# Sliding-window attention in a fused encoder layer: 128 key slots for every query chunk, weights divided before their transposes, values as the stationary operand with 64 columns

## The chip, the cores and the metric

One core of one Trainium2 chip. The metric is the device time of one execution in microseconds, as the median of several runs. TensorE multiplies, ScalarE and VectorE do the elementwise work, GpSimd makes constants at the start, SyncE issues the weight transfers. Everything is float32; the large products are made of rounded float32 parts (fp32r), one pass each, the small ones in plain float32, two passes each (transposes one).

## The reference, cut to what matters

One layer over 256 positions of width 2048: an input projection, a gated recurrence, the attention below, an output projection, an MLP, a gated embedding, norms. The change touches the attention alone.

```python
def swa_sink_attention(q, k, v, sinks, cos, sin):
    ...
    kb = band_blocks(k.reshape(B, N, CHUNK, ATT_KV_HEADS, ATT_HEAD_DIM), N)
    vb = band_blocks(v.reshape(B, N, CHUNK, ATT_KV_HEADS, ATT_HEAD_DIM), N)
    s = jnp.einsum('bnqhgd,bnkhd->bnhgqk', q, kb).astype(jnp.float32) * (ATT_HEAD_DIM ** -0.5)
    ...
    sink = jnp.broadcast_to(...)
    pr = jax.nn.softmax(jnp.concatenate([s, sink], axis=-1), axis=-1)[..., :-1].astype(v.dtype)
    o = jnp.einsum('bnhgqk,bnkhd->bnqhgd', pr, vb)
    return o.reshape(B, S, ATT_WIDTH)
...
merged = jnp.concatenate([jax.nn.sigmoid(gate_a) * o_a, jax.nn.sigmoid(gate_b) * o_b], axis=-1)
```

CHUNK is 64, a query sees the keys of its own chunk and of the one before (the first chunk only its own). There are 32 query heads of width 64 and 4 key and value heads, eight query heads to each.

## The kernel before, in words

**The stream.** All weights pass through TensorE in chunks of 2 x 128 rows by 512 columns. SyncE loads a chunk into one of 4 raw slots. ScalarE rounds it to `w_hi` (L893), VectorE makes the rest `w_lo` (L1220), and TensorE does 12 matmuls of 512 columns with it: four L641 and four L642 in turn (`w_hi` with the high and the low part of the activations), then four L647 (`w_lo`). There are 588 chunks; blocks of 8 or 4 chunks fill one pair of accumulators. ScalarE may split chunk n once TensorE has used chunk n-4, so each split waits for TensorE and the chunks follow each other without a gap as long as nothing is late.

**The steps.** All else is hung on that stream by a list of turns written out by hand: `steps(n)` on each engine. TensorE does the steps of turn n behind chunk n. ScalarE does them behind its split of chunk n+3 and VectorE behind its `w_lo` of chunk n+3 (`LAG` is 3). Every engine executes strictly in its written order, so a step that waits holds up all that is behind it, the splits too.

**The attention.** The 32 query heads are done in 4 groups j, each with one key head and in 8 units u: query tile t = u // 4 (128 queries, that is two chunks) and a pair of heads. Unit u of a group starts at turn `a = 4u + 4` of the group:

- a = 4u+4: TensorE, `scores` (L686). The stationary operand is `qT` of the two heads (128 columns are the 128 queries), the moving one `kTp`, in which the key head lies twice, each copy zero in the rows of the other head. Tile 0 sees keys 0 to 127 (256 moving columns), tile 1 keys 64 to 255 (384).
- a = 4u+5: VectorE, `score_max` (L1309, L1314, L1316), a reduction for each half of the rows, then the larger of it and the sink, negated. ScalarE, `exponentials` (L947), one for each half of the rows and head, four in all, into `pr0` or `pr1`.
- a = 4u+7: TensorE, `weights_turn` (L699), two transposes of 128x128 in tile 0, four in tile 1.
- a = 4u+8: VectorE copies them to `pT` (L1372).
- a = 4u+9: TensorE, `weighted_values` (L710), `pT` stationary, the values `vaug` moving with 64 columns and a 65th of ones that gives the sum of the weights.
- a = 4u+10: VectorE copies the output to `oa` (L1377).

Behind the last unit (`ATT_END`, a = 39) ScalarE makes the sinks' exponentials (L1000) and VectorE the denominators, the division and the product with the gate `sgb` (`attention_gated`, L1324 to L1330); TensorE transposes the result (`amT`), ScalarE and VectorE split it into `mT_hi` and `mT_lo` for the output projection.

The turns of TensorE share four PSUM banks; scores have bank 0, the transposed weights and the outputs of a unit bank 1. A turn waits until the one before it in its bank has been read.

**What runs beside it.** The recurrence has its steps in the same turns. Two of them matter below: its outputs (turn h = 47), where TensorE does 16 full-width matmul passes (L753), and 12 matmuls of two passes (L759) whose stationary operand has 64 columns:

```python
for h in range(HG):
    for c in (1, 2, 3):
        t, half = divmod(c, 2)
        mm = pe.matmul(bank(("o", j, t))[half * CHUNK:(half + 1) * CHUNK, h * P:(h + 1) * P],
                       qe[:, h, c * CHUNK:(c + 1) * CHUNK], Sst[:, c - 1, h, :],
```

so that c = 1 and 3 write output rows 64 to 127, c = 2 rows 0 to 63; and the split of its gated output (turn h = 62), of which VectorE's part is L1457. The latter falls among the first attention turns of the next group in group 1, in the others behind them. Turn h is counted from the block "f" of the group, a from the end of its block "gb"; both are the same chunk.

## Time and profile before

| | us |
|---|---|
| median of 3 runs | 1774.04 |
| lowest, highest | 1773.59, 1774.26 |
| span of the profiled execution | 1771.0 |
| TensorE matmuls busy | 1742.1 (98%) |
| VectorE busy | 1088.2 (61%) |
| ScalarE busy | 910.4 (51%) |

The span runs from the first to the last instruction of one profiled execution; the page gives no time of that execution besides it. The median of the runs is 3.0 us above it. Busy is the union of an engine's instructions. Matmuls overlap in the records, since each is written with its latency; the distance between the starts of two chunks, and not the mean length of a matmul, tells what one costs.

### The profile page before, as it was taken

The numbers are of one execution on the slowest core, as the hardware profiler recorded it, in microseconds if no ns is written. First come the engines' busy times: TensorE is split into PE (matmuls) and PEld (weight loads), VectorE is DVE, ScalarE is ACT, GpSimd is POOL, SyncE is SP. The second block draws the span as 40 slices with busy tenths as digits, with TensorE's granted clock in tenths as the row PEclk, the third lists the DMA queues.
The fourth block names the chain that finished last, engine by engine and source line by source line (L and its number), as shares of the span: only waits on it lengthen the run. The fifth ranks groups of instructions, "written<-read, shape, count | busy, mean of one in ns | idle before, by whom it ended". The sixth has DMA issues, their size and how long they took to land.

```text
span 1771.0 us, 22971 instructions
## 1 busy us (share of the span) xinstructions
PE 1742.1 (98%) x8357; PEld 1442.6 (81%) x8357; DVE 1088.2 (61%) x1432; ACT 910.4 (51%) x1160; POOL 21.9 (1%) x80
## 2 busy tenths in 40 slices
PE   7999999999999999999999999999999999999996
PEld 6888788888888888888888888888888888888885
DVE  6656776776657767577676455555555555555564
ACT  6556646554556545565456544444444444444453
POOL 4000000000000000000000000000000000000000
PEclk9999999999999999999999999999999999999998
DMA  6655555555655556555556666666666666666553
GB/s 217 200 171 174 155 155 177 166 160 157 188 181 163 165 155 189 180 167 160 157 184 208 188 181 192 187 192 188 189 183 194 185 191 189 191 186 184 176 185 113
DMA packets 162716, 315.33 MB, mean 178 GB/s; under 512 B 10097, under 2 KB 10418, under 8 KB 162482
## 3 DMA queue, kind: packets, MB, share of 16 engines
q1 hardware_dynamic: 161584, 312.01, 59.0%
q10 hardware_dynamic: 1026, 1.87, 0.3%
q8 instruction: 72, 1.18, 0.3%
q14 instruction: 34, 0.28, 0.1%
HBM read 311.74 MB, written 2.10 MB: 177 GB/s over the span
## 4 chain that ended last, share of the span: by engine, by line
PE 96%; DVE 1%; ACT 1%; issue 0%; DMA 0%; SPq 0%; DVEq 0%; ACTq 0%
PE acc L641 30%; PE acc L642 30%; PE acc L647 30%; PE turn L668 3%; PE turn L710 1%; PE turn L686 1%; PE turn L740 1%; PE turn L699 1%; DVE w_lo L1220 0%; ACT w_hi L893 0%; PE turn L759 0%; PE turn L753 0%; DMA w_raw<-in_w_in_dram 0%; PE turn L724 0%; DVE x_sb L1297 0%
## 5 line engine op out<-in xcount | busy, mean ns | idle before, releaser
L1220 DVE TENSOR_TENSOR w_lo<-w_raw,w_hi 128x1024 fp32r<-128x1024 f32 x588 | 719.9, 1224 | 619.3 <-ACT w_hi L893 615.5
L893 ACT ACTIVATE w_hi<-w_raw 128x1024 fp32r<-128x1024 f32 x588 | 623.1, 1060 | 699.1 <-PE acc L647 690.5
L641 PE MATMUL acc<-w_hi,hT_hi 128*128 128x512 f32 x1568 | 624.5, 398 | 6.9 <-ACT w_hi L893 3.9
L642 PE MATMUL acc<-w_hi,hT_lo 128*128 128x512 f32 x1568 | 611.9, 390 | 0.0
L647 PE MATMUL acc<-w_lo,hT_hi 128*128 128x512 f32 x1568 | 420.5, 390 | 0.0
L641 PEld LDWEIGHTS acc<-w_hi,hT_hi 128*128 128x128 f32 x1568 | 295.0, 188 | 69.5 <-ACT w_hi L893 4.3
L647 PEld LDWEIGHTS acc<-w_lo,hT_hi 128*128 128x128 f32 x1568 | 294.9, 188 | 61.8
L642 PEld LDWEIGHTS acc<-w_hi,hT_lo 128*128 128x128 f32 x1568 | 295.3, 188 | 59.1
L641 PE MATMUL acc<-w_hi,mT_hi 128*128 128x512 f32 x512 | 205.6, 401 | 0.0
L642 PE MATMUL acc<-w_hi,mT_lo 128*128 128x512 f32 x512 | 199.7, 390 | 0.0
L647 PE MATMUL acc<-w_lo,mT_hi 128*128 128x512 f32 x512 | 137.3, 390 | 0.0
L647 PEld LDWEIGHTS acc<-w_lo,mT_hi 128*128 128x128 f32 x512 | 96.1, 188 | 20.3
L641 PEld LDWEIGHTS acc<-w_hi,mT_hi 128*128 128x128 f32 x512 | 96.2, 188 | 19.7
L642 PEld LDWEIGHTS acc<-w_hi,mT_lo 128*128 128x128 f32 x512 | 96.3, 188 | 19.5
L641 PE MATMUL acc<-w_hi,aT_hi 128*128 128x512 f32 x256 | 100.7, 393 | 0.0
L642 PE MATMUL acc<-w_hi,aT_lo 128*128 128x512 f32 x256 | 100.0, 391 | 0.0
L947 ACT ACTIVATE pr<-turn,asc 64x128 f32<-64x128 f32 (+1 forms) x128 | 37.7, 343 | 96.6 <-DVE asc L1316 96.2
L647 PE MATMUL acc<-w_lo,aT_hi 128*128 128x512 f32 x256 | 69.0, 391 | 0.0
L1297 DVE TENSOR_TENSOR x_sb<-acc,x_sb 128x512 f32<-128x512 f32 x102 | 65.6, 685 | 1.8
L647 PEld LDWEIGHTS acc<-w_lo,aT_hi 128*128 128x128 f32 x256 | 48.1, 188 | 10.7
L642 PEld LDWEIGHTS acc<-w_hi,aT_lo 128*128 128x128 f32 x256 | 48.1, 188 | 10.3
L641 PEld LDWEIGHTS acc<-w_hi,aT_hi 128*128 128x128 f32 x256 | 48.1, 188 | 10.2
(210 smaller groups left out, 918.1 us busy)
## 6 DMA issues: line engine op xcount, KB each, us to landing
w_raw<-in_w_in_dram SPq DMA_DIRECT2D x232, 512.0 KB, 3.7
w_raw<-in_w_up_dram SPq DMA_DIRECT2D x128, 512.0 KB, 3.7
w_raw<-in_w_down_dram SPq DMA_DIRECT2D x128, 512.0 KB, 3.8
w_raw<-in_w_out_dram SPq DMA_DIRECT2D x64, 512.0 KB, 4.4
w_raw<-in_w_ple_gate_dram SPq DMA_DIRECT2D x32, 512.0 KB, 4.5
x_sb<-in_x_dram SPq DMA_DIRECT2D x8, 256.0 KB, 7.4
w_raw<-in_w_ple_proj_dram SPq DMA_DIRECT2D x4, 512.0 KB, 4.1
out_dram<-x_sb SPq DMA_DIRECT2D x3, 512.0 KB, 4.6
```

Source lines behind the costliest of these rows:

```text
L641: pe.matmul(a, hi[:, k, t, :], w_hi[:, s, kk, :], start=first and kk == 0, stop=False)
L642: pe.matmul(a, lo[:, k, t, :], w_hi[:, s, kk, :], start=False, stop=False)
L647: mm = pe.matmul(acc[b % 2][t][:], hi[:, k, t, :], w_lo[:, s, kk, :], start=False, stop=last and kk == 1)
L668: mm = pe.transpose(bank(name)[:, i * P:(i + 1) * P], src(i), ident[:])
L686: mm = pe.matmul(bank(name)[:, 0:2 * nk].rearrange("p (v k) -> p v k", v=2), qT[:, pair, t, :], kTp[:, j, :, k0:k0 + nk], start=True, stop ...
L699: mm = pe.transpose(bank(name)[:, i * P:(i + 1) * P], src, ident[:])
L710: mm = pe.matmul(bank(name)[:, hh * (HD + 1):(hh + 1) * (HD + 1)], pT[:, hh * (t + 1) + kt, :], vaug[:, kt, j, :], start=kt == 0, stop=kt ...
L740: mm = pe.matmul(bank(name)[:, h * P:(h + 1) * P], ke[:, h, c // 2, :], val[:, c // 2, h * P:(h + 1) * P], start=True, stop=True)
L893: act.activation(w_hi[:, n % W_SLOTS], w_raw[:, n % RAW_SLOTS], ACT.Copy)\
L947: ins = act.activation(dst, bank(name)[rows_, s0:s0 + keys], ACT.Exp, scale=HD ** -0.5, bias=asc[rows_, NM + head:NM + head + 1])
L1220: dve.tensor_tensor(w_lo[:, n % W_SLOTS], w_raw[:, n % RAW_SLOTS], w_hi[:, n % W_SLOTS].bitcast(F32), ALU.subtract).then_inc(w_lo_ready, 1)
L1297: dve.tensor_tensor(xs, acc_of(kind, j, col, t)[:], xs, ALU.add).then_inc(x_added, 1)
```

## The change

Each query chunk now has 128 key slots of its own. `kTp` has 5 pieces of 64 keys: chunks 0, 1, 2, then 1 and 3 again. For the second query chunk of tile 1 the keys are the pieces 2 and 4. The values `vv` have three tiles: the positions 0 to 127, 128 to 255, and a mixed one (the values of positions 128 to 191 in rows 0 to 63, of 64 to 127 in rows 64 to 127). `pr0` and `pr1` have 129 columns a head; the last holds the exponential of the sink. So in tile 1 every query has 128 keys: one reduction, one exponential a head over all 128 rows, two transposes.

The weights are divided before they are transposed: a new step `weights_normed` on VectorE at turn a = 4u+6 sums `pr` with the sink's column, takes the reciprocal and multiplies. TensorE's transposes wait for it (`pn_ready`) instead of for the exponentials.

The product with the values has the values stationary (64 columns) and the transposed weights moving, head 0 into rows 0 to 63 of the bank and head 1 into rows 64 to 127, so the output comes out turned (`oaT`). The gate is transposed instead of the gated output (`gbT`, turn 39 instead of 43), one product is left, and the split into `mT_hi` and `mT_lo` reads its result. The scores of tile 1 are two matmuls with 64 stationary columns.

```diff
-                k0, nk = keys_of(t)
-                mm = pe.matmul(bank(name)[:, 0:2 * nk].rearrange("p (v k) -> p v k", v=2),
-                               qT[:, pair, t, :], kTp[:, j, :, k0:k0 + nk], start=True, stop=True)
+                out_ = bank(name)[:, 0:2 * P].rearrange("p (v k) -> p v k", v=2)
+                if t == 0:
+                    mm = pe.matmul(out_, qT[:, pair, 0, :], kTp[:, j, :, 0:P], start=True, stop=True)
+                else:
+                    pe.matmul(out_[0:CHUNK], qT[:, pair, 1, 0:CHUNK], kTp[:, j, :, P:2 * P], start=True, stop=True,
+                              skip_group_check=True)
+                    late = kTp[:, j, :, P:5 * CHUNK].rearrange("p v (s c) -> p v s c", c=CHUNK)[:, :, 0:3:2, :]
+                    mm = pe.matmul(out_[CHUNK:P].rearrange("p v (s c) -> p v s c", c=CHUNK),
+                                   qT[:, pair, 1, CHUNK:P], late, start=True, stop=True, skip_group_check=True)
                 mm.then_inc(full(name), 1)
...
-                pe.wait_ge(pr_ready, 8 * j + u + 1)
+                pe.wait_ge(pn_ready, 8 * j + u + 1)
                 signal, value = bank_free(name)
                 pe.wait_ge(signal, value)
+                pr = pr0 if t == 0 else pr1
                 for hh in range(2):
-                    for kt in range(t + 1):
-                        i = hh * (t + 1) + kt
-                        src = pr0[:, hh, :] if t == 0 else pr1[:, hh, kt * P:(kt + 1) * P]
-                        mm = pe.transpose(bank(name)[:, i * P:(i + 1) * P], src, ident[:])
+                    mm = pe.transpose(bank(name)[:, hh * P:(hh + 1) * P], pr[:, hh, 0:P], ident[:])
...
-                for hh in range(2):
-                    for kt in range(t + 1):
-                        mm = pe.matmul(bank(name)[:, hh * (HD + 1):(hh + 1) * (HD + 1)],
-                                       pT[:, hh * (t + 1) + kt, :], vaug[:, kt, j, :],
-                                       start=kt == 0, stop=kt == t)
+                parts_ = ((0, slice(0, P)),) if t == 0 else ((V_MIXED, slice(0, CHUNK)), (V_LATE, slice(CHUNK, P)))
+                for v, qs in parts_:
+                    for hh in range(2):
+                        mm = pe.matmul(bank(name)[hh * HD:(hh + 1) * HD, qs], vv[:, v, j, :], pT[:, hh, qs],
+                                       start=True, stop=True, skip_group_check=True)
...
+                pr = pr0 if t == 0 else pr1
+                for hh in range(2):
+                    head = t * 8 + 2 * pair + hh
+                    act.activation(pr[:, hh, P:P + 1], sink_bc[:, 8 * j + 2 * pair + hh:8 * j + 2 * pair + hh + 1],
+                                   ACT.Exp, bias=asc[:, NM + head:NM + head + 1])
+                    for rows_, keys in parts_of(t):
+                        ins = act.activation(pr[rows_, hh, 0:keys], bank(name)[rows_, hh * P:hh * P + keys], ACT.Exp,
+                                             scale=HD ** -0.5, bias=asc[rows_, NM + head:NM + head + 1])
...
+            def weights_normed(j, u, t):
+
+                dve.wait_ge(pr_ready, 8 * j + u + 1)
+                pr, den = pr0 if t == 0 else pr1, asc[:, DEN:DEN + 2]
+                chain(dve.tensor_reduce(den, pr[:], AX_X, ALU.add))
+                chain(dve.reciprocal(den, den))
+                dve.tensor_tensor(pr[:, :, 0:P], pr[:, :, 0:P], den.unsqueeze(2).to_broadcast([P, 2, P]), ALU.mult)\
+                   .then_inc(pn_ready, 1)
...
+                        if a == UNIT * u + 6:
+                            weights_normed(j, u, t)
...
-                    if a == ATT_END + 2:
-                        dve.wait_ge(pv_out, 8 * (j + 1))
-                        dve.wait_ge(gb_sig, 2 * (j + 1))
-                        attention_gated(j)
+                    if a == ATT_END + 1:
+                        dve.wait_ge(pv_out, 8 * (j + 1))
+                        for t in range(TT):
+                            dve.wait_ge(full(("gbT", j, t)), nth(("gbT", j, t)))
+                            dve.tensor_tensor(four(sgb[:, t]), oaT[:, :, t, :], four(bank(("gbT", j, t))[:]), ALU.mult)\
+                               .then_inc(am_ready, 1)
```

Here `parts_of(t)` gives the halves of the rows with 64 and 128 keys in tile 0 and all rows with 128 keys in tile 1. Line numbers move: L1220 becomes L1226, L893 L897, L699 L703, L947 L948 with the sinks' L945, L1377 L1375; the new three are L1325 to L1327. The changes of order, as the built programs have it:

VectorE, unit 2 of group 1 (tile 0), from the bound of the scores to the recurrence's scan (`hb`); before:

```order
L1309 TENSOR_REDUCE asc<-turn 64x2 x2
L1314 SCALAR_TENSOR_TENSOR asc<-asc,sink_bc 128x2
L1316 TENSOR_SCALAR asc<-asc 128x2
L1494 TENSOR_SCALAR hk<-hf 128x512
L1220 TENSOR_TENSOR w_lo<-w_raw,w_hi 128x1024
L1377 COPY oa<-turn 128x130
L1500 SCALAR_TENSOR_TENSOR hb<-smask,hg 128x512
```

and after:

```order
L1311 TENSOR_REDUCE asc<-turn 64x2 x2
L1316 SCALAR_TENSOR_TENSOR asc<-asc,sink_bc 128x2
L1318 TENSOR_SCALAR asc<-asc 128x2
L1487 TENSOR_SCALAR hk<-hf 128x512
L1226 TENSOR_TENSOR w_lo<-w_raw,w_hi 128x1024
L1375 COPY oaT<-turn 128x128
L1325 TENSOR_REDUCE asc<-pr 128x2
L1326 RECIPROCAL asc<-asc 128x2
L1327 TENSOR_TENSOR pr<-pr,asc 128x2x128
L1493 SCALAR_TENSOR_TENSOR hb<-smask,hg 128x512
```

Three instructions have come in behind the copy of the last output, and the one that TensorE's transposes wait for is the third.

ScalarE, the exponentials of a unit of tile 0 and what stands behind them, after (before it was four of L947 in one row, in the order of the halves):

```order
L945 ACTIVATE pr<-sink_bc,asc 128x1
L948 ACTIVATE pr<-turn,asc 64x64
L948 ACTIVATE pr<-turn,asc 64x128
L945 ACTIVATE pr<-sink_bc,asc 128x1
L948 ACTIVATE pr<-turn,asc 64x64
L948 ACTIVATE pr<-turn,asc 64x128
L1060 ACTIVATE hg<-hf 128x512
```

Six instead of four, and the rows change from one to the next: all, the first 64, the last 64.

TensorE, scores of a unit of tile 1 with the recurrence's transposes behind it; before:

```order
L647 MATMUL acc<-w_lo,hT_hi 128x512 x4
L686 MATMUL turn<-kTp,qT 128x384
L668 MATMUL turn<-ident,zb 128x128 x4
L641 MATMUL acc<-w_hi,hT_hi 128x512
L642 MATMUL acc<-w_hi,hT_lo 128x512
```

and after:

```order
L647 MATMUL acc<-w_lo,hT_hi 128x512 x4
L689 MATMUL turn<-kTp,qT 64x256
L692 MATMUL turn<-kTp,qT 64x256
L668 MATMUL turn<-ident,zb 128x128 x4
L641 MATMUL acc<-w_hi,hT_hi 128x512
```

One matmul over 384 columns has become two over 256, each for half of the output rows.

## Rows read from the trace of the kernel before

**Rows 1.** The page, part 4: the chain that ended last, by engine.

```profile
PE 96%; DVE 1%; ACT 1%; issue 0%; DMA 0%; SPq 0%; DVEq 0%; ACTq 0%
```

**Rows 2.** Timeline of PE, tile 0 of group 3: start us, us, engine, line, operands.

```profile
742.37 1.07 PE L647 MATMUL acc<-w_lo,hT_hi 128*128 128x512 f32 x4
745.09 1.07 PE L647 MATMUL acc<-w_lo,hT_hi 128*128 128x512 f32 x4
...
748.07 1.09 PE L647 MATMUL acc<-w_lo,hT_hi 128*128 128x512 f32 x4
...
751.26 1.08 PE L647 MATMUL acc<-w_lo,hT_hi 128*128 128x512 f32 x4
...
754.45 1.07 PE L647 MATMUL acc<-w_lo,hT_hi 128*128 128x512 f32 x4
```

**Rows 3.** Timeline of PE, tile 1 of group 3: transposes, scores; then a values step.

```profile
809.94 1.07 PE L647 MATMUL acc<-w_lo,mT_hi 128*128 128x512 f32 x4
...
813.13 1.08 PE L647 MATMUL acc<-w_lo,hT_hi 128*128 128x512 f32 x4
...
816.52 1.07 PE L647 MATMUL acc<-w_lo,hT_hi 128*128 128x512 f32 x4
...
829.13 1.08 PE L647 MATMUL acc<-w_lo,hT_hi 128*128 128x512 f32 x4
...
832.77 1.07 PE L647 MATMUL acc<-w_lo,hT_hi 128*128 128x512 f32 x4
```

**Rows 4.** Timeline of PE, recurrence outputs of group 0; last row: the instant 240.30.

```profile
238.41 1.95 PE L753 MATMUL turn<-val,am 128*128 128x128 f32 x16
240.29 1.96 PE L759 MATMUL turn<-Sst,qe 128*64 128x128 f32 x24
...
242.52 0.39 PE L642 MATMUL acc<-w_hi,hT_lo 128*128 128x512 f32 x1
...
240.29 0.33 PE L759 MATMUL turn<-Sst,qe 128*64 128x128 f32 x2
```

**Rows 5.** Timelines of DVE, ACT and PE, unit 2 of group 3.

```profile
752.61 0.17 DVE L1316 TENSOR_SCALAR asc<-asc 128x2 f32<-128x2 f32 x1
...
752.93 1.14 ACT L947 ACTIVATE pr<-turn,asc 64x64 f32<-64x64 f32 x4 [2.60 <-DVE asc L1316]
...
757.04 0.29 DVE L1377 COPY oa<-turn 128x130 f32<-128x130 f32 x1
...
758.08 0.38 PE L699 MATMUL turn<-ident,pr 128*128 128x128 f32 x2
```

**Rows 6.** Timelines of DVE and PE: units 1, 0 and 4 of group 3, unit 0 of group 1.

```profile
743.94 0.29 DVE L1377 COPY oa<-turn 128x130 f32<-128x130 f32 x1
...
731.17 2.48 DVE L1220 TENSOR_TENSOR w_lo<-w_raw,w_hi 128x1024 fp32r<-128x1024 f32 x2 [2.43 <-ACT w_hi L893]
...
733.52 0.38 PE L699 MATMUL turn<-ident,pr 128*128 128x128 f32 x2
...
781.81 0.29 DVE L1377 COPY oa<-turn 128x130 f32<-128x130 f32 x1
...
782.85 0.60 PE L699 MATMUL turn<-ident,pr 128*128 128x128 f32 x4
...
288.06 0.69 DVE L1457 TENSOR_TENSOR mT_lo<-tmp,mT_hi 128x512 fp32r<-128x512 f32 x1 [0.48 <-ACT mT_hi L1105]
...
288.09 0.38 PE L699 MATMUL turn<-ident,pr 128*128 128x128 f32 x2
```

**Rows 7.** Groups by line and form, DVE and ACT: xcount, busy us, mean ns, idle before.

```profile
L1309 DVE TENSOR_REDUCE asc<-turn 64x2 f32<-64x256 f32 x48 | 20.4, 424 | 1.7
...
L947 ACT ACTIVATE pr<-turn,asc 64x128 f32<-64x128 f32 x96 | 29.6, 356 | 53.9 <-DVE asc L1316 53.5
...
L947 ACT ACTIVATE pr<-turn,asc 64x64 f32<-64x64 f32 x32 | 8.1, 303 | 42.7 <-DVE asc L1316 42.7
...
L1000 ACT ACTIVATE asc<-asc 128x16 f32<-128x16 f32 x4 | 0.9, 217 | 0.1
```

More of the change, by code:

```diff
@@ L974, in steps @@
                         act.wait_ge(full(("kT", i)), nth(("kT", i)))
[L975 to L977 removed]
+                        src = bank(("kT", i))[:].rearrange("p (h v c) -> p h v c", h=2, v=2)
+                        pieces = ((0, 0, 2), (1, 3, 1)) if t == 0 else ((0, 2, 1), (1, 4, 1))
+                        for c, slot_, n_ in pieces:
+                            ins = act.activation(
+                                kTp[:, 2 * half:2 * half + 2, :, slot_ * CHUNK:(slot_ + n_) * CHUNK],
+                                src[:, :, :, c * CHUNK:(c + n_) * CHUNK], ACT.Copy)
+                        ins.then_inc(kTp_out, 1)
                 for j in range(NG):
@@ L987, in steps @@
                     if a == 0:
+                        if j:
+                            act.wait_ge(moA_ready, 2 * j)
                         z_out("gb", j, sgb, gb_exp, ACT.Exp, NR)
@@ L1302, in score_max @@
                 dve.wait_ge(full(name), nth(name))
-                k0, nk = keys_of(t)
-                s = bank(name)[:, 0:2 * nk].rearrange("p (v k) -> p v k", v=2)
-                for half in range(2):
-                    rows_ = slice(half * CHUNK, (half + 1) * CHUNK)
-                    first = max(0, (2 * t + half - 1) * CHUNK) - k0
-                    end = (2 * t + half + 1) * CHUNK - k0
-                    chain(dve.tensor_reduce(asc[rows_, MX:MX + 2], s[rows_, :, first:end], AX_X, ALU.max))
+                s = bank(name)[:, 0:2 * P].rearrange("p (v k) -> p v k", v=2)
+                for rows_, keys in parts_of(t):
+                    chain(dve.tensor_reduce(asc[rows_, MX:MX + 2], s[rows_, :, 0:keys], AX_X, ALU.max))
                 head = 2 * pair
```

93 lines of the change are left out of this document (28 added, 65 removed).

## Prediction, made before the changed kernel ran

> **What bounds the kernel now.** I read the page first, then its chain of work, then the timelines of three engines in the attention turns. The chain that ended last is TensorE for 96% of the span [rows 1]. So the time is the sum of what TensorE executes plus the moments in which it waits, and every edit has one of two prices: its TensorE time, or a late operand.
>
> The price of a piece is read between chunks. A chunk ends with four L647 matmuls; from one such start to the next is 2.72 us when nothing lies between (742.37 to 745.09), and what is above 2.72 is the piece [rows 2]. In query tile 0: two transposes of weights 0.26 (2.98), scores 0.47 (3.19), values 0.47 (3.19) [rows 2]. In tile 1: four transposes 0.47 (3.19), scores over 384 columns 0.67 (3.39), values in eight passes 0.92 (829.13 to 832.77, 3.64) [rows 3].
>
> **TensorE, part by part.** There are 4 groups of 8 units, 16 units in each tile.
> The transposes of tile 1 fall from four to two: 0.47 becomes 0.26, 16 x -0.21 = -3.4 us.
> Scores of tile 0 keep their form: 0.
> Scores of tile 1 and all products with the values become 64 columns wide, in the two halves of the array. The kernel has one such step, the recurrence outputs (L759), and its price is in the trace [rows 4]. The 16 full-width L753 passes of 128 columns take 1.95 us in their row. The 24 half-width L759 passes behind them, of the same 128 columns, take 1.96; 16 of the 24 fall on the upper half and 8 on the lower. A view of the instant 240.30 has two of them from the same start, 240.29. So the halves run together, and the eight of the lower half cost nothing. A pass of 128 columns is 0.11 (two more transposes cost 0.21 [rows 2, 3]) and one of L641's 2.72/12 = 0.23. From 238.41 to the next L642 at 242.52 are 4.11; the work in it is 16 x 0.11 + 16 x 0.11 + 0.23 = 3.75. What is left, 0.35 us, is the price of a visit to the halves, going in and coming out.
> Scores of tile 1: two passes of 256 columns, 0.43, plus 0.35 = 0.78 for 0.67: 16 x 0.11 = +1.8.
> Values of tile 0: two passes of 128 columns a half, 0.22+0.35 = 0.57 for 0.47: 16 x 0.10 = +1.6.
> Values of tile 1: four passes of 64 columns a half, at 0.055 again 0.22+0.35 = 0.57 for 0.92: 16 x -0.35 = -5.6. No row has a 64-column load at this rate; at 0.11 a pass it would be 0.79. I take 0.57, since L759's loads were hidden, and keep +3.5 us for the range.
> The transposes of the gate are as many as those of the gated output that they replace: 0. The sum for TensorE is -3.4+1.8+1.6-5.6 = -5.6 us.
>
> The Trainium skill (TensorE: Matmul & The Clock Gate, "The mechanism" of Part 3) says that a load overlaps with matmuls in flight only when its row group differs. The halves here share all their rows, so by that rule they would go in turn; the trace disagrees, with the two starts at 240.29. What it would give is the third rival below.
>
> **ScalarE and VectorE, and the new wait.** The transposes of a unit (chunk 4u+7 of its group) waited for the exponentials; now they wait for VectorE's sum, reciprocal and product behind them (chunk 4u+6). All three engines are in order, so what stands before them counts: the unit's exponentials hold up the next weight split on ScalarE, that holds up VectorE's w_lo, and behind it come the copy of the last output and then the three new instructions, w_lo of the next chunks behind those.
> The new three: 0.42 (a 64x256 reduction [rows 7]; the product has 256 elements too), about 0.17 for two elements (as L1316 [rows 5]), 0.42, with 0.04 between: 1.09; to TensorE's first transpose another 0.15. ScalarE's part in tile 0: four exponentials take 1.14 [rows 5]; two sink exponentials are added (217 ns for 16 columns [rows 7]) and the order now changes the rows used at each step. A 64x128 one is 356 ns and a 64x64 one 303 [rows 7]; six one after another without overlap make 2 x (0.22+0.30+0.36) = 1.76, with some 0.01 at each joint 1.83: +0.69. If all five joints overlap by 0.1 they make 1.26: +0.12. I take +0.69: of today's four, 2 x (0.30+0.36) = 1.32 less 1.14 leaves 0.18, an overlap at two of three joints; the third is the one at which the rows change, and now every joint changes them. In tile 1 four become two of 128 columns and two sinks: shorter by about 0.3.
> Unit 0 of a group: the first w_lo ends 731.17+1.22 (half of 2.48, with its gap) = 732.40, the turn was at 733.52, 1.12 later [rows 6]. Needed are 0.69+0.03+1.09+0.15 = 1.96: TensorE waits 0.8, in three groups 2.4.
> Unit 0 of group 1: VectorE was busy with mT_lo until 288.06+0.69 = 288.75, already behind the turn at 288.09 [rows 6]; 288.75+0.69+1.09+0.15-288.09 = 2.6.
> Unit 2: last bound (L1316) 752.78, exponentials from 752.93, copy of the output done at 757.33, turn at 758.08: 0.75 left [rows 5]. Needed: 0.69+1.09-0.09+0.15 = 1.84, less 0.10 by which the longer product before it delays TensorE: 1.0, four times 4.0.
> Units 1 and 3: the copy is done at 743.94+0.29 = 744.23 and the turn follows four L647 passes of 0.23 from 745.09, at 746.0 [rows 2, 6]; 1.77 are left and 1.84 less 0.10 needed: 0.
> Unit 4: copy done 782.10, turn 782.85, 0.75 left [rows 6]; 1.15 needed and part of tile 0's lateness still there: 0.4 to 0.9, I take 0.6, four times 2.4.
> Units 5 to 7: VectorE is freed of one reduction (424 ns [rows 7]) and half a copy in each, which pays for most of the new three: 0.
> Waits: 2.4+2.6+4.0+2.4 = +11.4 us. These are what the change costs; the old tail at the end of a group (sum of denominators, 16 exponentials, four products of 512) goes, but nothing waited for it: 0. The extra pieces of kTp and values are some 0.3 us each, once, in slots where ScalarE waits for TensorE: 0. No weight transfer changes.
>
> **Sum.** 1771.0-5.6+11.4 = 1776.8 us for the span. The median of the runs (1774.04) lies 3.0 above the profiled span; the page gives no other time of that execution. So 1779.8, rounded 1780. A measurement of this kernel tells about 0.2%, 3.5 us, from no change: +6 is slower by 0.34%.
>
> **Rivals.**
> First, the new three are mostly covered: the six exponentials overlap (+0.12), so each wait of tile 0 shrinks by 0.57, 7 x 0.57 = 4.0 us, and unit 4 costs 0.4, 0.8 less. 1780-4.8 = 1775: no change that can be told. For it: two of the three joints of today's four do overlap [rows 5, 7]; against: copies then still end 0.75 before the turn.
> Second, faster: VectorE's slack holds the whole chain, TensorE never waits, and only -5.6 is left: 1768.4. It decides at 1.1 us between the copy's end and the turn; rows 5 and 6 have 0.75, which is against it. The same side is reached if visits to the halves are free: 48 x 0.35 = 16.8 us less, while 32 turns come up to 0.35 earlier and waits grow by 5 to 11: about 1770. The 0.35 around L759 is against it. The Trainium skill (TensorEngine Tiling (Array Packing), "When to Use Tiling") advises just this exchange, values stationary and two column tiles for 64 columns, for up to twice the speed; its key properties add that a change of mode drains the engine. By that gain alone the values' 0.47 and 0.92 would halve and the kernel end near 1770; the rows say that the drain eats it.
> Third, the halves go in turn: +0.43 for each scores step of tile 1, +0.22 for each product with the values, 6.9+7.0 = 13.9, less some 2 us of waits that the longer TensorE work covers: 1792. Rows 4 are against it.
> Fourth, the change could do nothing (the wait moved, all hidden, and the pieces equal): 1774. Nothing in the rows supports it.
>
> **From this the numbers.** My forecast (waits in units 0, 2 and 4) 0.62; the first rival 0.18; the second 0.10; the third 0.06; the fourth 0.04. The range reaches from the lower end of the first rival to the forecast with slow loads (+3.5) and waits larger by 0.3 in 15 places (+4.5): 1772 to 1788. Slower by over 0.2%: 0.62, the third rival and a part of the first, less the forecast's lower edge: 0.67. Within: 0.23. Faster: 0.10.
>
> **What would show it.** In the profile after: TensorE's idle time at the transposes of weights, put down to VectorE's product (L1327), about 11 us in some 13 to 16 pieces, the longest (2 to 2.6) in group 1 near 290 us; scores of tile 1 3.5 from chunk to chunk instead of 3.39, values about 3.3 in both tiles; two transposes in tile 1. The six exponentials of a tile 0 unit take 1.8. I am wrong if TensorE's waits there are under 6 us in all, or if a values step costs more than 0.7.

## The result and the profile after

The changed kernel takes 1782.65 us (median of 4 runs, 1782.08 to 1783.13) against 1773.99 us of the kernel before in the same session: the ratio is 1.005, with a 95% interval of 1.0038 to 1.0062. It is slower by half a per cent, as forecast (1780, range 1772 to 1788). The profiled execution took 1782.92 us, with a span of 1780.8, so what lies around that span is 2.1 us.

The page of the changed kernel, parts 1 and 4, which answer to [rows 1]:

```profile
PE 1741.2 (98%) x8357; PEld 1418.8 (80%) x8357; DVE 1097.0 (62%) x1492; ACT 913.7 (51%) x1194; POOL 21.8 (1%) x79
...
PE 85%; DVE 8%; ACT 4%; issue 1%; DMA 0%; ACTq 0%; SPq 0%; DVEq 0%
```

The chain that ended last was TensorE for 96% of the span; now VectorE has 8% of it and ScalarE 4%. The list of waits says where (engine, line, what was waited for: us in total, times, longest):

```profile
PEld turn L703 <- DVE pr L1327: 19.7, 18, 2.7
PE turn L703 <- DVE pr L1327: 11.2, 11, 2.3
PE turn L703 <- ACT w_hi L897: 1.2, 1, 1.2
```

L703 are the transposes of the weights, L1327 is the product of the division. Eleven times TensorE stood idle for it, and once more (the 1.2 us of the last row, unit 2 of group 0) with the releaser put down to ScalarE's w_hi of the same moment.

Three timelines show one such place, unit 2 of group 3, as [rows 5] did before (start us, duration us, engine, line, operands; in brackets the idle time and its releaser). VectorE, then ScalarE, then TensorE:

```profile
762.39 0.17 DVE L1318 TENSOR_SCALAR asc<-asc 128x2 f32<-128x2 f32 x1
...
766.31 1.23 DVE L1226 TENSOR_TENSOR w_lo<-w_raw,w_hi 128x1024 fp32r<-128x1024 f32 x1 [3.42 <-ACT w_hi L897]
767.57 0.29 DVE L1375 COPY oaT<-turn 128x128 f32<-128x128 f32 x1
767.78 0.41 DVE L1325 TENSOR_REDUCE asc<-pr 128x2 f32<-128x258 f32 x1
768.23 0.17 DVE L1326 RECIPROCAL asc<-asc 128x2 f32<-128x2 f32 x1
768.43 0.43 DVE L1327 TENSOR_TENSOR pr<-pr,asc 128x256 f32<-128x256 f32 x1
...
762.72 0.29 ACT L945 ACTIVATE pr<-sink_bc,asc 128x1 f32<-128x1 f32 x1 [3.09 <-DVE asc L1318]
762.92 0.67 ACT L948 ACTIVATE pr<-turn,asc 64x64 f32<-64x64 f32 x2
763.61 0.29 ACT L945 ACTIVATE pr<-sink_bc,asc 128x1 f32<-128x1 f32 x1
763.92 0.69 ACT L948 ACTIVATE pr<-turn,asc 64x64 f32<-64x64 f32 x2
764.63 0.63 ACT L1060 ACTIVATE hg<-hf 128x512 f32<-128x512 f32 x1
765.17 2.14 ACT L897 ACTIVATE w_hi<-w_raw 128x1024 fp32r<-128x1024 f32 x2
...
766.63 1.07 PE L647 MATMUL acc<-w_lo,hT_hi 128*128 128x512 f32 x4
768.91 0.44 PE L703 MATMUL turn<-ident,pr 128*128 128x128 f32 x2 [1.21 <-DVE pr L1327]
```

Read it as a chain. The bound ends at 762.56. ScalarE's six exponentials end at 764.61, 2.05 us later (before: 1.30 [rows 5]). They hold up w_hi, that holds up w_lo, and VectorE reaches the output's copy (L1375) only at 767.57. Behind it stand the three new instructions, 767.78 to 768.86. TensorE had issued its last L647 pass and waited 1.21 us.

TensorE's pieces in tile 1 of group 3, as in [rows 3]:

```profile
821.40 1.07 PE L647 MATMUL acc<-w_lo,mT_hi 128*128 128x512 f32 x4
822.31 0.38 PE L703 MATMUL turn<-ident,pr 128*128 128x128 f32 x2
824.38 1.08 PE L647 MATMUL acc<-w_lo,hT_hi 128*128 128x512 f32 x4
825.39 0.43 PE L689 MATMUL turn<-kTp,qT 128*64 128x256 f32 x1
825.40 0.43 PE L692 MATMUL turn<-kTp,qT 128*64 128x256 f32 x1
...
827.93 1.07 PE L647 MATMUL acc<-w_lo,hT_hi 128*128 128x512 f32 x4
828.93 0.45 PE L715 MATMUL turn<-pT,vv 128*64 128x64 f32 x8
831.25 1.07 PE L647 MATMUL acc<-w_lo,hT_hi 128*128 128x512 f32 x4
```

Two transposes: 2.98 from L647 to L647; scores in halves: 3.55; values in halves: 3.32. The two scores passes, one a half, start 0.01 us apart.

Two sums over the whole trace close the account. I took the time from each chunk's start to the next and subtracted the plain 2.72. By kind, against before: transposes -3.5, scores +1.8, values -3.5, so TensorE's own work is 5.2 us less (the waits are out of this). What a chunk with transposes took beyond its transposes is 16.3 us, against 2.6 before: +13.7. And one chunk, behind the longest wait, grew by 1.6 for another reason (last section). -5.2+13.7+1.6 = +10.1; the spans differ by 9.8. (A chunk is measured here from the first L642 of one to the first L642 of the next, and two transposes are taken at 0.22.)

### The profile page after: what moved, and what is told of

Read it like the earlier page. It is cut to its first block, busy times and chain, and to the rows that moved or that the text cites. A ratio compares the mean times of both kernels' runs of the same rounds, so it can differ in the third digit from the quotient of the medians.

```text
span 1780.8 us, 23060 instructions
## 1 busy us (share of the span) xinstructions
PE 1741.2 (98%) x8357; PEld 1418.8 (80%) x8357; DVE 1097.0 (62%) x1492; ACT 913.7 (51%) x1194; POOL 21.8 (1%) x79
## 4 chain that ended last, share of the span: by engine, by line
PE 85%; DVE 8%; ACT 4%; issue 1%; DMA 0%; ACTq 0%; SPq 0%; DVEq 0%
PE acc L641 27%; PE acc L642 27%; PE acc L647 26%; DVE w_lo L1226 4%; PE turn L668 2%; ACT w_hi L897 2%; ACT pr L948 1%; DVE asc L1311 1%; PE turn L744 1%; DVE pr L1327 0%; DVE x_sb L1303 0%; PE turn L763 0%; PE turn L703 0%; PE turn L757 0%; PE turn L715 0%
## 5 line engine op out<-in xcount | busy, mean ns | idle before, releaser
L1226 DVE TENSOR_TENSOR w_lo<-w_raw,w_hi 128x1024 fp32r<-128x1024 f32 x588 | 720.0, 1224 | 619.7 <-ACT w_hi L897 616.3
L897 ACT ACTIVATE w_hi<-w_raw 128x1024 fp32r<-128x1024 f32 x588 | 622.7, 1059 | 696.0 <-PE acc L647 687.8
L642 PE MATMUL acc<-w_hi,hT_lo 128*128 128x512 f32 x1568 | 612.9, 391 | 0.0
L647 PE MATMUL acc<-w_lo,hT_hi 128*128 128x512 f32 x1568 | 420.0, 390 | 0.0
L647 PEld LDWEIGHTS acc<-w_lo,hT_hi 128*128 128x128 f32 x1568 | 295.1, 188 | 62.1
L642 PEld LDWEIGHTS acc<-w_hi,hT_lo 128*128 128x128 f32 x1568 | 295.5, 188 | 58.8
L642 PE MATMUL acc<-w_hi,mT_lo 128*128 128x512 f32 x512 | 199.9, 390 | 0.0
L647 PE MATMUL acc<-w_lo,mT_hi 128*128 128x512 f32 x512 | 137.1, 389 | 0.0
L647 PEld LDWEIGHTS acc<-w_lo,mT_hi 128*128 128x128 f32 x512 | 96.1, 188 | 20.4
L642 PEld LDWEIGHTS acc<-w_hi,mT_lo 128*128 128x128 f32 x512 | 96.2, 188 | 18.9
L642 PE MATMUL acc<-w_hi,aT_lo 128*128 128x512 f32 x256 | 100.0, 391 | 0.0
L647 PE MATMUL acc<-w_lo,aT_hi 128*128 128x512 f32 x256 | 69.0, 391 | 0.0
L945 ACT ACTIVATE pr<-sink_bc,asc 128x1 f32<-128x1 f32 x64 | 18.7, 292 | 89.5 <-DVE asc L1318 78.2
L647 PEld LDWEIGHTS acc<-w_lo,aT_hi 128*128 128x128 f32 x256 | 48.1, 188 | 10.7
L642 PEld LDWEIGHTS acc<-w_hi,aT_lo 128*128 128x128 f32 x256 | 48.1, 188 | 10.4
```

The costliest lines, as they stand in the source:

```text
L642: pe.matmul(a, lo[:, k, t, :], w_hi[:, s, kk, :], start=False, stop=False)
L647: mm = pe.matmul(acc[b % 2][t][:], hi[:, k, t, :], w_lo[:, s, kk, :], start=False, stop=last and kk == 1)
L897: act.activation(w_hi[:, n % W_SLOTS], w_raw[:, n % RAW_SLOTS], ACT.Copy)\
L945: act.activation(pr[:, hh, P:P + 1], sink_bc[:, 8 * j + 2 * pair + hh:8 * j + 2 * pair + hh + 1], ACT.Exp, bias=asc[:, NM + head:NM + head ...
L1226: dve.tensor_tensor(w_lo[:, n % W_SLOTS], w_raw[:, n % RAW_SLOTS], w_hi[:, n % W_SLOTS].bitcast(F32), ALU.subtract).then_inc(w_lo_ready, 1)
```

## The experiments

All were made from the changed kernel unless another is named. Medians in us; the ratio is to the kernel before, run on the same chip.

| run | what | median | ratio, 95% interval |
|---|---|---|---|
| e1_turn_later | transposes and all behind them one chunk later | 1774.95 | 1.0005 (0.9996-1.0014) |
| e2_no_norm | no division | 1766.84 | 0.9962 (0.9949-0.9976) |
| e3_norm_aside | division made, not waited for | 1773.05 | 0.9994 (0.9985-1.0003) |
| e4_rows_in_order | exponentials by rows | 1776.28 | 1.0014 (1.0005-1.0024) |
| e5_copy_earlier | e1, copy of unit 1 earlier | 1769.46 | 0.9974 (0.9964-0.9984) |
| e6_visits_together | values beside scores | 1802.57 | 1.0163 (1.0149-1.0177) |
| e7_one_half | e5, values in one half | 1773.14 | 0.9996 (0.9987-1.0006) |
| e8_values_twice | e5, values twice | 1772.12 | 0.9992 (0.9983-1.0001) |
| e9_spread_together | new timetable | 1760.08 | 0.9920 (0.9906-0.9933) |
| e10_aside_last | e3, the three last in their step | 1768.05 | 0.9965 (0.9952-0.9979) |
| e11_before_spread | kernel before on e9's timetable | 1769.42 | 0.9976 (0.9966-0.9986) |
| e12_norm_last_odd | changed kernel, the three last in units 1, 3 | 1780.17 | 1.0037 (1.0024-1.0050) |

### Is it the division? e2_no_norm and e3_norm_aside

```diff
-                pe.wait_ge(pn_ready, 8 * j + u + 1)
+                pe.wait_ge(pr_ready, 8 * j + u + 1)
...
-                        if a == UNIT * u + 6:
-                            weights_normed(j, u, t)
```

> The sum, the reciprocal and the product of the weights are left out, so the weights stay undivided, and the transposes wait for the exponentials alone, at their old place. Theory: 1.09 us of the chain in front of each transpose goes; what is left is ScalarE's 0.75 us longer chain in tile 0, which fits the slack. TensorE keeps only the change of its forms, -4.5 us against before, and the 2.5 us that before too waited in the first groups: 1769 to 1771 us. Rival (the six exponentials are the cause and the division rides along): units 0 and 2 still wait 0.3 us or more each, 1773 or more. Rival 2 (the 64-column forms cost more than they save): within 3 us of after.

Measured 1766.84, 15.8 below the changed kernel and 6.9 below the one before. That is 2.2 below my 1769 to 1771: TensorE's forms save 5.2 and not 4.5, and of the old waits, which I took to stay at 2.5, 1.3 us are left. The exponentials alone make no wait to speak of, and the new forms do save: the rivals that blamed ScalarE or the 64-column forms are out.

e3 keeps VectorE's three instructions and removes only the wait:

```diff
-                pe.wait_ge(pn_ready, 8 * j + u + 1)
+                pe.wait_ge(pr_ready, 8 * j + u + 1)
...
-                dve.tensor_tensor(pr[:, :, 0:P], pr[:, :, 0:P], den.unsqueeze(2).to_broadcast([P, 2, P]), ALU.mult)\
+                dve.tensor_tensor((pr1 if t == 0 else pr0)[:, :, 0:P], pr[:, :, 0:P], den.unsqueeze(2).to_broadcast([P, 2, P]), ALU.mult)\
```

> VectorE does the same three instructions in the same place, but the product goes to a buffer that nobody reads (that of the other query tile) and the transposes wait only for the exponentials: the weights that are used stay undivided. It parts the wait for the division from VectorE's load. Theory (the wait is the cost): 1769 to 1772 us, since w_lo of the chunk has about 1 us to spare. Rival (VectorE's load is the cost, by making w_lo or the copies late): over 1776 us, with idle time at L647 or at the products with the values, put down to VectorE.

1773.05: a little above my 1769 to 1772 and far from the rival's 1776. So 9.6 us are the wait for the division, and 6.2 us (e3 against e2) are VectorE's load, which I had at nothing. Where do they fall? In units 2 and 4, and not on L647: the transposes wait there for the copy of the output of the unit before (its list of waits has PE turn L703 for DVE oaT L1375, 4.7 us in 8 times).

### Where the load acts: e10_aside_last

Timelines of VectorE, ScalarE and VectorE again in e3, from the division of unit 1 of group 3 to the copy that unit 2's transposes need:

```profile
746.23 0.43 DVE L1327 TENSOR_TENSOR pr<-pr,asc 128x256 f32<-128x256 f32 x1
746.57 0.42 DVE L1476 TENSOR_SCALAR hf<-hf 128x512 f32<-128x512 f32 x1
...
747.09 0.63 ACT L1053 ACTIVATE hf<-hf 128x512 f32<-128x512 f32 x1 [1.43 <-DVE hf L1476]
...
753.90 0.17 DVE L1318 TENSOR_SCALAR asc<-asc 128x2 f32<-128x2 f32 x1
...
759.08 0.29 DVE L1375 COPY oaT<-turn 128x128 f32<-128x128 f32 x1
```

The division of unit 1 stands ahead of a clamp of the recurrence (L1476). ScalarE waits 1.43 us for that clamp, with w_hi behind it, so w_lo, the bound of unit 2, its exponentials and the next w_hi all come late, and so the copy L1375. The complete changed kernel has the same wait in its unit 1 of group 3, on ScalarE:

```profile
755.57 0.63 ACT L1053 ACTIVATE hf<-hf 128x512 f32<-128x512 f32 x1 [1.42 <-DVE hf L1476]
```

Transposes and outputs share one PSUM bank (bank 1), so the transposes of a unit need that copy. The Trainium skill (PSUM — Partial Sum Buffer, "PSUM bank collisions raise a hardware error") says that two engines must not be on one bank in the same partitions at once, which would forbid dropping this wait; no run here shows what dropping it does. Putting the three behind the clamp tests the reading:

```diff
-                        if a == UNIT * u + 6:
-                            weights_normed(j, u, t)
...
                     for hp in range(2):
                         pair_steps(j, hp, h)
+                    for u in range(8):
+                        if a == UNIT * u + 6:
+                            weights_normed(j, u, u // 4)
```

> As e3_norm_aside (the product goes aside, nobody waits for it), but the three instructions stand last in VectorE's step of that chunk, behind the recurrence's instructions of the same step. It asks where the 6.2 us come from that VectorE's load alone cost there. Theory: in unit 1 the three stand ahead of the clamp (L1476) for which ScalarE's next two instructions and then its w_hi wait; that makes w_hi, w_lo, the bound of unit 2 and with it the copy of the output late, which the transposes of unit 2 need because of the shared bank. Behind the clamp they delay none of that: the waits at unit 2 (0.5 to 1.3 us) and 4 (0.3 to 0.9) shrink by half or more, 1768 to 1770 us. Rival (VectorE is simply busy for longer, wherever the three stand): 1772 to 1774 us.

1768.05, 5.0 of the 6.2 us back with the same work done. The timeline of ScalarE in e10 shows its wait for the clamp (now L1477) at 0.43 in place of 1.43:

```profile
741.89 0.63 ACT L1053 ACTIVATE hf<-hf 128x512 f32<-128x512 f32 x1 [0.43 <-DVE hf L1477]
```

It is the place in the queue, not the busy time. The same edit on the complete changed kernel, in units 1 and 3 alone:

```diff
-                        if a == UNIT * u + 6:
+                        if u not in (1, 3) and a == UNIT * u + 6:
...
+                    for u in (1, 3):
+                        if a == UNIT * u + 6:
+                            weights_normed(j, u, 0)
```

> The changed kernel, complete, with one edit: in units 1 and 3 VectorE's three new instructions stand behind the recurrence's instructions of the same step (the clamps L1476 and L1500), not ahead of them. Theory (a part of the waits at units 2 and 4 is VectorE's load ahead of those clamps, 5 us in all by the two runs with the product put aside; the rest is the division's own length): the wait at unit 4 (0.9 us in three groups) nearly goes, that at unit 2 (1.45) shrinks by 0.5 to 1.0, those at units 0 stay: 1777 to 1780 us. Rival (the waits are the division's own length alone): 1782 to 1783.

1780.17, just outside my 1777 to 1780. Per group the wait at unit 4 went (0.89 to 0), that at unit 2 fell from 1.45 to 0.95, but units 1 and 3, whose division is now last in its step, wait some 0.3 and 0.45 (0 and 0.1 to 0.2 without the edit). Here the product is needed, and being last has its own price.

### Exponentials by rows: e4_rows_in_order

```diff
-                for hh in range(2):
-                    head = t * 8 + 2 * pair + hh
-                    act.activation(pr[:, hh, P:P + 1], sink_bc[:, 8 * j + 2 * pair + hh:8 * j + 2 * pair + hh + 1],
-                                   ACT.Exp, bias=asc[:, NM + head:NM + head + 1])
-                    for rows_, keys in parts_of(t):
...
+                for rows_, keys in parts_of(t):
+                    for hh in range(2):
+                        head = t * 8 + 2 * pair + hh
+                        act.activation(pr[rows_, hh, 0:keys], bank(name)[rows_, hh * P:hh * P + keys], ACT.Exp,
+                                       scale=HD ** -0.5, bias=asc[rows_, NM + head:NM + head + 1])
+                for hh in range(2):
+                    head = t * 8 + 2 * pair + hh
+                    ins = act.activation(pr[:, hh, P:P + 1], sink_bc[:, 8 * j + 2 * pair + hh:8 * j + 2 * pair + hh + 1],
+                                         ACT.Exp, bias=asc[:, NM + head:NM + head + 1])
```

> The same six exponentials of a unit, ordered by rows: those of the lower rows for both heads, those of the upper rows for both heads, the two sinks last. In tile 0 the rows then change twice in place of five times. Theory (each change of rows costs ScalarE the overlap of two neighbours, and the first sink starts 0.2 us later behind the bound than an exponential of scores does): first start to last end falls from 1.68 to 1.5 and the start behind the bound from 0.36 to 0.16, so each of the some 12 waits at the transposes shrinks by 0.3 to 0.4 us: 1778 to 1780 us. Rival (the joints do not depend on the rows, and the sinks cost the same wherever they stand): within 1 us of after, 1782 to 1783.

That text misreads one number: 0.36 was the start of the first exponential of scores, behind the sink; the sink itself starts 0.16 behind the bound (762.56 to 762.72 above). The measure: 1776.28, 6.4 below the changed kernel and 1.7 below my 1778 to 1780 (its profiled execution, at 1779.29, was the slowest of ten). ScalarE, unit 2 of group 3:

```profile
758.95 1.14 ACT L946 ACTIVATE pr<-turn,asc 64x64 f32<-64x64 f32 x4 [2.69 <-DVE asc L1320]
760.10 0.48 ACT L950 ACTIVATE pr<-sink_bc,asc 128x1 f32<-128x1 f32 x2
```

Six in 1.63 us in place of 1.89. The four take 1.14 as before the change, and the two sinks overlap by 0.1. In these rows and in [rows 5] two neighbours overlap where both start at the same row, and not where the next starts at another. That is not a whole rule: in the changed kernel the second sink (763.61, 0.29 long) and the exponential behind it (763.92) both start at row 0 and do not overlap, in any of the 16 units of tile 0, while the first sink and the one behind it do (762.72 and 762.92). What decides there stays open. The waits at the transposes fell from 16.3 to 10.3 us; the spans of the two profiled executions differ by 3.6 only, of which e4's start takes 1.4 (its second chunk begins at 19.44 us and that of the changed kernel at 18.01).

### One chunk later: e1_turn_later and e5_copy_earlier

```diff
-                        if a == UNIT * u + 7:
+                        if a == UNIT * u + 8:
                             weights_turn(j, u, t)
-                        if a == UNIT * u + 9:
+                        if a == UNIT * u + 10:
                             weighted_values(j, u, t)
...
-                        if a == UNIT * u + 8:
+                        if a == UNIT * u + 9:
                             dve.wait_ge(full(("pT", j, u)), nth(("pT", j, u)))
...
-                        if a == UNIT * u + 10:
+                        if a == UNIT * u + 11:
                             dve.wait_ge(full(("pv", j, u)), nth(("pv", j, u)))
```

> The transposes of the weights, the copy of the turned weights, the products with the values and the copy of the outputs all come one chunk (2.72 us) later in their unit; nothing else changes. Theory (TensorE waits because the division comes late, and its new forms save 4.5 us beside that): the waits in front of the transposes were 16.3 us in all (excess over a plain chunk, less 0.22 for each pair of transposes) and at most 2.5 us each, so a chunk more covers every one of them: 13 to 16 us less than after, 1767 to 1770 us, and faster than before by 4 to 7 us; idle time at L703 under 1 us. Rival 1 (the new forms cost more than the chunks show, and the waits only stand where something else would stand anyway): at most 5 us less than after, 1778 or more, with new idle time at the products with the values or at the next scores. Rival 2 (VectorE's added work makes w_lo late, wherever the transposes stand): idle time moves to L647, 1775 or more.

A miss: 1774.95, 5 us above my range's end. The waits for L1327 are gone, all of them. New ones stand at unit 2 of each group. Timeline of TensorE, then of VectorE, e1, group 3:

```profile
764.76 0.41 PE L703 MATMUL turn<-ident,pr 128*128 128x128 f32 x2 [1.57 <-DVE oaT L1375]
...
761.21 1.22 DVE L1493 TENSOR_TENSOR_SCAN hb<-smask,hg 128x512 f32<-128x512 f32 x1
762.46 0.69 DVE L1495 TENSOR_TENSOR hd<-hb 128x512 f32<-128x512 f32 x1
763.07 1.22 DVE L1226 TENSOR_TENSOR w_lo<-w_raw,w_hi 128x1024 fp32r<-128x1024 f32 x1
764.32 0.29 DVE L1375 COPY oaT<-turn 128x128 f32<-128x128 f32 x1
```

Again the shared bank: the copy moved behind the scan. One more edit puts that one copy ahead of it:

```diff
-                        if a == UNIT * u + 11:
+                        if a == UNIT * u + (10 if u == 1 else 11):
```

> The late turn of the first run, with one more edit: VectorE copies the output of unit 1 one chunk earlier, ahead of its scan for the recurrence. Theory: the transposes of a unit use the same PSUM bank as the outputs of the unit before, so they wait for the copy of these too; in the first run that copy stood behind w_lo, the three new instructions and the scan of 1.22 us, and TensorE waited 1.76, 3.50, 2.03 and 1.75 us at unit 2 of the four groups, 9.0 in all. They fall under 0.3 each, and the kernel comes to 1766 to 1768 us. Rival (the late turn costs that time by itself, because ScalarE's and VectorE's chains are too long for a unit): unit 2 still waits a microsecond or more in each group, 1771 or more.

1769.46, 1.5 above my range. The waits at unit 2 are gone; 3.9 us are there, 0.6 at unit 7 of group 0 as in e1, the others at units 3 and 4, where e1 had none and I expected none. This kernel is faster than the one before by 0.26%.

### What a step in halves costs: e7_one_half and e8_values_twice

```diff
-                        mm = pe.matmul(bank(name)[hh * HD:(hh + 1) * HD, qs], vv[:, v, j, :], pT[:, hh, qs],
+                        mm = pe.matmul(bank(name)[0:HD, hh * P + qs.start:hh * P + qs.stop], vv[:, v, j, :], pT[:, hh, qs],
```

> As e5_copy_earlier, but the second head's product with the values goes to the same half of the array as the first's, into other columns, so the two can't run side by side; the second head's output is left out. Theory (the two halves run together, the lower one is free): a values step grows from 0.60 by 0.22, 32 steps, +7.0 us against e5_copy_earlier: 1773 to 1775 us. Rival (the halves go in turn anyway): no change in the step, 1766 to 1768.

```diff
-                for v, qs in parts_:
+                for v, qs in parts_ + parts_:
```

> As e5_copy_earlier, but each products-with-the-values step is issued twice in a row, with the same result. It parts the price of a step (0.60 us) into what each pass costs and what the visit costs. Theory (0.22 to 0.25 for the passes, 0.35 for the visit): +0.22 to 0.25 a step, 32 steps, +7 to +8 us: 1773 to 1776 us. Rival 1 (the halves go in turn): +0.44 a step, +14 us: 1780 to 1782. Rival 2 (the passes themselves are slow, there is no price of a visit): +0.60 a step, +19 us: 1785 to 1787.

Timeline of TensorE in e8, tile 1 of group 3:

```profile
832.90 1.07 PE L647 MATMUL acc<-w_lo,hT_hi 128*128 128x512 f32 x4
833.89 0.69 PE L715 MATMUL turn<-pT,vv 128*64 128x64 f32 x16
836.46 1.07 PE L647 MATMUL acc<-w_lo,hT_hi 128*128 128x512 f32 x4
```

3.56 from L647 to L647 in place of 3.32, and over the 28 steps that stand alone in their turn the median goes from 3.30 (e5) to 3.53, in both runs. So a step is 0.23 of passes and 0.37 of visit, and one half alone takes twice the 0.23: the halves run together, in tile 0 and tile 1. The Trainium skill (TensorE: Matmul & The Clock Gate, "The mechanism" of Part 3) says that a load overlaps with matmuls in flight only when its row group differs; taken by itself this would put the halves in turn, and these rows are against it. The times rose by 3.7 (e7, 1773.14) and 2.7 (e8, 1772.12), not 7: the longer steps covered 3 us of the waits that e5 still had. So e8 missed its range by 0.9, and e7 met 1773 to 1775 by luck, since e5, from which both start, had ended above its own range. The reading rests on the chunks, not on the two times.

### Sharing a visit: e6_visits_together and e9_spread_together

```diff
-                        if a == UNIT * u + 7:
+                        if a == UNIT * u + 9:
                             weights_turn(j, u, t)
-                        if a == UNIT * u + 9:
+                        if a == UNIT * u + (12 if u < 7 else 11):
                             weighted_values(j, u, t)
```

with this line set ahead of scores, the exponentials at 4u+6, the division at 4u+7, the copies at 4u+10 and 4u+13.

> The units are spread over more chunks, so that the products with the values of unit u stand directly ahead of the scores of unit u+2 in the same turn: exponentials one chunk later, division one later, transposes two later, products with the values three later. In four of these pairs of each group both steps are 64 columns wide. Theory (0.35 us is the price of a visit to the halves, whatever is done in it): a chunk with values and scores of tile 1 is 3.8 us instead of 4.1, 16 x 0.35 = 5.6 us less than the run before it, 1761 to 1763 us if nothing waits. Rival 1 (the 0.35 belongs to each step, not to the visit): the chunk is 4.1 and the time that of the run before it, 1766 to 1768. Rival 2 (the order brings new waits, ScalarE for the copy of the turned weights): idle time at L703 or L945's followers, over 1768.

1802.57, and yet the first theory is right in its chunk. Timeline of TensorE, tile 1 of group 3:

```profile
837.05 1.07 PE L647 MATMUL acc<-w_lo,hT_hi 128*128 128x512 f32 x4
838.05 0.45 PE L715 MATMUL turn<-pT,vv 128*64 128x64 f32 x8
...
838.56 0.38 PE L692 MATMUL turn<-kTp,qT 128*64 128x256 f32 x1
840.82 1.07 PE L647 MATMUL acc<-w_lo,hT_hi 128*128 128x512 f32 x4
845.32 0.41 PE L703 MATMUL turn<-ident,pr 128*128 128x128 f32 x2 [3.44 <-DVE oaT L1375]
```

Values and scores together: 3.77 from L647 to L647 (median of chunks 3.73), where apart they would make 3.33+3.53-2.72 = 4.14. A shared visit saves some 0.40. It is the visit and not the neighbourhood: in tile 0, where the scores are full-width (L687), the shared chunk has a median of 3.72, and the two apart (3.16 to 3.19 and 3.30) would make 3.74 to 3.77. The last row is what ruined it: the transposes at 4u+9 need the copy of the output of unit u-1 out of their bank, and that stands at 4(u-1)+13, the same chunk. There were 16 such waits, 29.7 us, the longest 4.2.

e9 gives every step a chunk in hand and puts the two copies ahead of w_lo:

```diff
-        ATT_END = UNIT * 7 + 11
+        ATT_END = UNIT * 7 + 13
...
+                        if a == UNIT * u + 12:
+                            weighted_values(j, u, t)
                         if a == UNIT * u + 4:
                             scores(j, u, t, pair)
-                        if a == UNIT * u + 7:
+                        if a == UNIT * u + 10:
                             weights_turn(j, u, t)
-                        if a == UNIT * u + 9:
-                            weighted_values(j, u, t)
...
-                        if a == UNIT * u + 5:
+                        if a == UNIT * u + 7:
                             exponentials(j, u, *divmod(u, 4))
...
+            def copies(n):
...
+                        if a == UNIT * u + 11:
+                            dve.wait_ge(full(("pT", j, u)), nth(("pT", j, u)))
...
+                        if a == UNIT * u + 13:
+                            dve.wait_ge(full(("pv", j, u)), nth(("pv", j, u)))
...
-                        if a == UNIT * u + 6:
+                        if a == UNIT * u + 8:
                             weights_normed(j, u, t)
...
+                copies(slot[0] - LAG)
                 split_lo(slot)
```

> The change with another timetable, built on what the runs before showed. A unit is spread over nine chunks: scores at 4u+4, bound at 4u+5, exponentials at 4u+7 (they no longer hold ScalarE up for the bound), division at 4u+8, transposes at 4u+10, products with the values at 4u+12, in one visit with the scores of unit u+2. The two copies out of the shared bank (turned weights at 4u+11, output at 4u+13) stand ahead of w_lo of their chunk, where VectorE was idle. Each step of a unit has at least one chunk in hand. Theory (what is left of e5_copy_earlier are about 4 us of waits in units 3 and 4, and 0.35 to 0.40 us for each visit that is shared, 16 of them with scores 64 columns wide): 1769.5-4-6 = 1759 us, 1757 to 1762. Rival (the copies ahead of w_lo make w_lo late, or the exponentials wait for the copy): idle time at L647 or new waits at L703, 1766 or more.

1760.08, 0.80% below the kernel before and 22.6 us below the changed one. The page's chain, e9:

```profile
PE 97%; DVE 1%; ACT 1%; DMA 0%; issue 0%; SPq 0%; DVEq 0%; ACTq 0%
```

No wait at L703 is left. The sum against the changed kernel: 16.3 us of waits, 1.6 of the chunk behind the longest, and 16 x 0.40 = 6.4 of visits make 24.3; the spans differ by 21.4. Of the 2.9 between, 1.0 stands in the first chunk, behind the loads of x, and 1.2 in chunks with nothing between; 0.7 I can't place. The profiled execution of e9 was the slowest of its five, 1.4 above their median.

### How much is the timetable? e11_before_spread

The kernel before with e9's edits (the same lines, its own copies).

> The kernel before (full-width forms, division at the end of the group) on the timetable of e9_spread_together. It asks how much of the 1760.08 us belongs to the timetable alone. Theory: the kernel before has only the 2.1 us wait of the first group (and 0.1 here and there) to lose, and its scores and values, both full width, save little by standing together (0.08 us where tile 0's scores did): 1770 to 1773 us, so that on this timetable the change is worth some 11 us. Rival (the timetable is the gain, by freeing ScalarE of its wait for the bound): 1766 or less.

1769.42, 0.6 below my range. Its span is 3.6 below that of before: 2.3 from waits and 1.0 from values beside scores. On this timetable the change makes the kernel 9.3 us faster, on the old one 8.7 slower: it lost by its place in the queues, not by its work.

## Why the prediction was right

The mechanism was the forecast one: TensorE's own work fell, and VectorE's division came late at units 0, 2 and 4. The size was near in part by luck: the term of the waits was too small by 2.3 us, the clock had no term, and the time around the span was put too high by about one.

- **TensorE's forms: -5.6 forecast, -5.2 measured.** Transposes -3.4 against -3.5, scores +1.8 against +1.8, values -4.0 against -3.5. A values step is 0.60 in both tiles; 0.57 was forecast. The visit of 0.35 is 0.37 by e8, and the second rival's free visit and the third's halves in turn are out by e7 and e8.
- **ScalarE: +0.69 forecast, +0.75 measured.** 1.83 was forecast for the six in tile 0, and 1.89 came: 762.72 to 764.61. A sink exponential took longer than its neighbour of 16 columns [rows 7], as the group by line says, but the first joint overlapped, which paid part of it. By group and form:

```profile
L945 ACT ACTIVATE pr<-sink_bc,asc 128x1 f32<-128x1 f32 x64 | 18.7, 292 | 89.5 <-DVE asc L1318 78.2 <-issue 11.1
```

- **The new three: 1.09 forecast, 1.08 measured** (767.78 to 768.86). To TensorE's first transpose I added 0.15; it was 0.05 (768.86 to 768.91).
- **The waits: +11.4 forecast, +13.7 measured.** Unit 0: 0.8 forecast, 0.83 measured. Unit 0 of group 1: 2.6 and 2.5. Unit 4: 0.6 and 0.89, though only in three of the groups. Unit 2: 1.0 and 1.45, the term that was mis-sized. I took the bound and the copy before the division as they stood before the change [rows 5], and let only ScalarE's 0.69 move them. But the bound, which ended 5.30 us before the turn (752.78 to 758.08), now ends 4.98 before the place that the turn would have without its wait (762.56 to 766.63+0.91; 0.91 is the distance from 821.40 to 822.31 above). e10 shows what moved it, the division of unit 1 ahead of a clamp, and in e12, with that moved away, unit 2 waits 0.95. "Units 5 to 7: 0" held, but for unit 7 of group 0, whose wait was 2.2 before the change, in the span that I started from, and is 1.6 now; and "units 1 and 3: 0" nearly (unit 3: 0.1 to 0.2).
- **What I had at nothing and was not:** VectorE's load. e3 against e2 gives it 6.2 us where the division isn't waited for; in the complete kernel part of it hides behind the wait, 2.5 us by e12.
- **Around the span:** I put 3.0 us there from the median; the changed kernel has 2.1. That made the forecast of the time a microsecond better than that of the span, which came out 4.0 above mine: 0.4 from the forms, 2.3 from the waits, 1.6 from the clock (4.3). That microsecond is the luck. In the later runs of the kernel before, each with its own span, time and span lie only 1.7 to 1.8 apart; my 3.0 held more than a microsecond by which the profiled execution was faster than the median. The clock is that of the last section.
- The first rival (a mostly covered division) was wrong as a whole. Its condition was six exponentials in 1.26 us; e4, one edit away, comes to 1.63.

## What to carry over

Before an instruction is put ahead of another on an in-order engine, look not only at who waits for the new one, but at who waits for what is now behind it: here a clamp, for which another engine waited with the main loop's work behind it. When a kernel has a timetable, a new link in a chain wants its own slot, and so does every copy out of a shared bank; the cheapest place for a copy was the idle time ahead of w_lo. And a saving should be priced by the visit, not by the pass: 0.37 of 0.60 us was entering and leaving.

## What the runs showed of the hardware

The longest wait cost more than its length. In group 1 of the changed kernel TensorE stood idle for 2.27 us, and then its matmuls came every 0.43 us in place of 0.23. Timeline of TensorE and its windows with the granted clock (window; length, PE busy, clock, DMA share, GB/s):

```profile
291.62 0.44 PE L703 MATMUL turn<-ident,pr 128*128 128x128 f32 x2 [2.27 <-DVE pr L1327]
...
293.54 0.63 PE L642 MATMUL acc<-w_hi,hT_lo 128*128 128x512 f32 x1
293.96 0.63 PE L641 MATMUL acc<-w_hi,hT_hi 128*128 128x512 f32 x1
```

```profile
290.00:292.00 2.00, 0.38 (x3) 1.00 0.63 226
292.00:293.00 1.00, 1.00 (x5) 0.73 0.00 0
293.00:294.00 1.00, 1.00 (x4) 0.50 0.24 35
294.00:295.00 1.00, 1.00 (x4) 0.50 0.82 213
295.00:296.00 1.00, 1.00 (x4) 0.56 0.84 307
296.00:297.00 1.00, 1.00 (x6) 1.00 0.94 248
```

The clock fell from its upper level of 2.4 GHz to 1.2 behind the idle stretch and came back near 296. The chunk behind the wait (292.12 to 296.89) took 4.77 us where its like take 3.20. The 1.21 us waits left the clock at 1.00, and so did the 2.0 us one of the kernel before (unit 7 of group 0); in e1 a wait of 2.49 us was followed by 0.50 again, and in e6, where several waits were over 3 us, the mean clock of the run is 0.991 against 0.997 of e9. So part of e6's loss is clock. Of the waits of one kernel the long one is the first to remove.
